# Conditioning pairs at other places, an attention step in another order, and a last step by halves

## The chip, the cores and the metric

The kernel runs on one NeuronCore of one Trainium2 chip, as one program. The metric is the time of the device in microseconds, lower is better; the kernel before took 2285.16 us, the median of three runs (2285.12 to 2285.46). Everything is float32 at the interface. A product in full precision is made as three matmuls of fp32r halves: the operand is split into a rounded part (`hi`, a cast on ACT) and the rest (`lo`, a subtraction on DVE).

## The reference

Two blocks are chained. x has 256 tokens and 1024 features.

```python
# first block
h = rms_norm(x, norm_mix)
u = h @ w_in                                   # short conv, NSA, gated delta net parts
branches = einsum('bsrc,rcd->bsrd', [y_a, y_n, y_g], w_branch)
gates    = sigmoid(h @ w_gate + b_gate)        # three branches, 1024 wide each
x = x + sum_r(gates * branches) @ w_out
x = x + hier_moe(rms_norm(x, norm_ffn), ...)   # 32 experts of 512
# second block: two layers with conditioning
mod = silu(c) @ ada_w + ada_b                  # per layer 6 x 1024: shift, scale, gate, twice
# layer 0: latent attention (MLA), 16 heads; gated FFN of 2816
# layer 1: state space (Mamba-2), 32 heads; 8 experts of 2816, 2 per token
#   x = x + gate * f(norm(x) * (1 + scale) + shift) for each of the four parts
out = rmsnorm(x, final_gain)
```

The NSA part of the first block has three attentions (compressed, selected blocks, window) over 8 heads, all with softmax over at most 256 keys.

## The kernel before

Each engine runs its own function per stage, one instruction stream each, and the streams meet only at semaphores; the order within a stream is written out by hand. Stages in order: the first block's norm, the convolution and the projections, the delta net (`gdn_*`), NSA (`nsa_*`), the merge of the branches (`merge_*`), the output projection (`proj_*`), the first mixture of experts, latent attention (`mla_*`), FFN (`ffn_*`), state space (`ssm_*`), the second mixture (`moe2`), the last norm (`last_*`).

**Weights** come through one ring of four slots (`Ring`, L103), 2 MB each. SP issues the loads in one fixed order, which is the order in which the units are written down (`columns_unit` L719, `ada_units` L724): the load of unit n waits until unit n − 4 has been emptied, and the loads behind it wait with it. A unit for a full-precision product is split into parts (`Split`, L157); `split.make_hi(a, n)` (cast, L192) and `split.make_lo(v, n)` (subtraction, L202) bring the split up to part n where they are called, and no part can be split beyond the buffers that PE has used.

**Conditioning pairs.** mod for one layer comes in 6 pairs. A pair is two ring units; `ada_pe` (L1198, its matmuls are L1209) multiplies it in 64 matmuls, `ada_act` copies the row out of PSUM (L1220), `ada_turn_pe` turns it into columns (4 small matmuls), and `ada_turn_dve` stores these into `mod_all` (L1235). There is one row buffer, so pair n + 1 is copied only when pair n is turned. In the first block's stages the pairs 3, 4 and 5 of layer 0 lie at the end of the delta net (3), after the first NSA unit (4) and ahead of the first scores (5), and pairs 1 to 5 of layer 1 in the steps 1, 3, 5, 7 and 8 of the latent attention's loop.

**Attention** (`attention_pe`, `attention_act` L1680, `attention_dve` L1703) is a loop over jobs n, shared by NSA and latent attention. ACT per step: exponentials of job n, then work put beside the loop (`beside`), then the copy of the turned probabilities of job n − 2 from PSUM (`pT`, L1700), for which PE waits before it multiplies them with the values. NSA's beside work is the merge: parts of the gates' and branches' products on PE, their hi and lo on ACT and DVE, and the gates' sigmoid (`gate_act`), which needs another activation table.

**Norms.** `norm_pe` (L922) fills PE's wait for a norm with products of constants, whose number is its last argument; `constant_products` does the same elsewhere. Their results aren't used. A norm's mean square is taken half on ACT, half on DVE; POOL makes the reciprocal root (L892, L893).

**The end.** The last down product's rows are scaled by DVE (L2448), split into hi and lo over 1024 columns, scattered to the tokens by matmuls (L252) and added to x (L2409), each an operation over the full width. Then comes the last norm, with both output tiles on DVE (L3994) and a store for each by SP.

## Time and profile before

| | us |
|---|---|
| Median of three runs | 2285.16 |
| Profiled execution, whole | 2277.89 |
| its span, first to last instruction | 2276.2 |
| PE busy in the span | 1946.6 (86%) |
| DVE busy | 1088.7 (48%) |
| ACT busy | 854.5 (38%) |
| POOL busy | 43.6 (2%) |
| Granted TensorE clock, mean | 0.955 |
| HBM read | 659.90 MB, 290 GB/s over the span |

| Stage | from | to |
|---|---|---|
| up to the projections | 0 | 112 |
| delta net | 112 | 255 |
| NSA | 255 | 423 |
| merge, output projection | 423 | 468 |
| first mixture | 470 | 952 |
| latent attention | 953 | 1117 |
| FFN | 1118 | 1319 |
| state space | 1320 | 1550 |
| second mixture | 1551 | 2267 |
| last norm | 2267 | 2276.2 |

The times of single instructions are those of the profiled execution. Idle time of an engine costs only what it delays at the next semaphore where the other engines are waiting already.

### The profile page before, as it was taken

What the parts mean: (1) busy time and instruction counts of PE and PEld (TensorE: products, weight loads), DVE (VectorE), ACT (ScalarE), POOL (GpSimd) and SP (SyncE); (2) the same over time, 40 slices, a digit from 0 to 9 for tenths busy, and PEclk for the clock granted to TensorE, in tenths of its full rate; (3) what the DMA queues carried; (4) which work ended last, traced back from release to release, by engine and by line L of the source; (5) the groups of instructions that cost most, each with busy time, mean ns of one, the idle gap of its engine ahead of it and who ended that gap; (6) DMA issues with size and microseconds to landing.
All of it is one profiled execution on the core that took longest, in us unless ns stands there. A gap on an engine that the chain in (4) does not pass through costs nothing.

```text
span 2276.2 us, 30142 instructions
## 1 busy us (share of the span) xinstructions
PE 1946.6 (86%) x12025; PEld 1394.2 (61%) x12025; DVE 1088.7 (48%) x1666; ACT 854.5 (38%) x1153; POOL 43.6 (2%) x111
## 2 busy tenths in 40 slices
PE   7989997996656666598899998998989998999997
PEld 7968776762111111266899898877665674664672
DVE  3845565432111110223555477876474573574572
ACT  4432345310000000234444357765463462463460
POOL 0010200000000000000000000000000000000000
PEclk9989998999889888899999999999999999999999
DMA  8563561579999999949555454445799999999996
GB/s 262 182 222 112 192 240 69 221 282 392 409 409 409 409 409 409 354 171 356 199 177 182 169 159 161 144 158 205 281 404 383 398 408 409 408 407 409 396 408 278
DMA packets 232012, 663.12 MB, mean 291 GB/s; under 512 B 24580, under 2 KB 33320, under 8 KB 231604
## 3 DMA queue, kind: packets, MB, share of 16 engines
q1 hardware_dynamic: 224108, 652.94, 75.4%
q10 hardware_dynamic: 7752, 8.11, 1.3%
q8 instruction: 101, 1.65, 0.3%
q14 instruction: 51, 0.42, 0.1%
HBM read 659.90 MB, written 1.10 MB: 290 GB/s over the span
## 4 chain that ended last, share of the span: by engine, by line
PE 54%; DMA 22%; DVE 13%; ACT 7%; issue 3%; POOL 0%; ACTq 0%; SPq 0%; DVEq 0%; POOLq 0%
PE psum L263 11%; PE psum L264 11%; PE psum L265 11%; PE psum L252 6%; DMA ring<-in_w_expert_down 5%; DMA ring<-in_w_expert_up 5%; DMA ring<-in_w_expert_gate 5%; PE psum L2506 4%; DMA ring<-in_moe_w_gate 3%; DVE w_lo L202 3%; PE psum L2802 3%; ACT w_hi L192 2%; PE psum L2560 2%; PE psum L1209 1%; DVE xbc L1008 1%
## 5 line engine op out<-in xcount | busy, mean ns | idle before, releaser
L202 DVE TENSOR_TENSOR w_lo<-ring,w_hi 128x1024 fp32r<-128x1024 f32 (+1 forms) x492 | 573.1, 1186 | 402.8 <-ACT w_hi L192 395.4
L192 ACT CAST w_hi<-ring 128x1024 fp32r<-128x1024 f32 (+1 forms) x492 | 497.3, 1020 | 381.2 <-PE psum L265 290.1
L2802 PE MATMUL psum<-ring,hT 128*32 128x512 f32 x960 | 147.1, 744 | 116.4 <-DMA ring<-in_w_expert_gate 63.4
L2802 PEld LDWEIGHTS psum<-ring,hT 128*32 128x32 f32 x960 | 30.3, 123 | 225.6 <-issue 88.1
L263 PE MATMUL psum<-w_hi,xg_hi 128*128 128x512 f32 (+1 forms) x384 | 147.1, 383 | 20.3 <-DVE w_lo L202 20.3
L2506 PE MATMUL psum<-ring,xg_pair 128*64 128x512 f32 (+1 forms) x768 | 155.1, 559 | 3.2 <-DMA ring<-in_moe_w_up 3.2
L2409 DVE TENSOR_TENSOR x<-x,psum 128x1024 f32<-128x1024 f32 x26 | 31.2, 1219 | 249.7 <-PE psum L252 249.7
L264 PE MATMUL psum<-w_hi,xg_lo 128*128 128x512 f32 (+1 forms) x384 | 145.1, 378 | 0.0
L265 PE MATMUL psum<-w_lo,xg_hi 128*128 128x512 f32 (+1 forms) x384 | 144.9, 377 | 0.0
L2506 PEld LDWEIGHTS psum<-ring,xg_pair 128*64 128x64 f32 x768 | 54.1, 137 | 98.9 <-issue 94.9
L2824 PE MATMUL psum<-ring,midT 128*32 128x512 f32 x480 | 69.2, 711 | 42.1 <-DMA ring<-in_w_expert_down 42.1
L263 PE MATMUL psum<-h_f_hi,w_hi 128*128 128x256 f32 x352 | 100.6, 286 | 1.8 <-DVE h_f_lo L920 1.8
L264 PE MATMUL psum<-h_f_hi,w_lo 128*128 128x256 f32 x352 | 100.4, 285 | 0.0
L265 PE MATMUL psum<-h_f_lo,w_hi 128*128 128x256 f32 x352 | 100.4, 285 | 0.0
L263 PEld LDWEIGHTS psum<-w_hi,xg_hi 128*128 128x128 f32 x384 | 73.0, 190 | 41.4 <-issue 27.7
L2560 PE MATMUL psum<-ring,midT 128*64 128x512 f32 x352 | 79.5, 596 | 7.0 <-DMA ring<-in_moe_w_down 7.0
L265 PEld LDWEIGHTS psum<-w_lo,xg_hi 128*128 128x128 f32 x384 | 72.9, 190 | 14.3
L264 PEld LDWEIGHTS psum<-w_hi,xg_lo 128*128 128x128 f32 x384 | 73.0, 190 | 13.6
L263 PE MATMUL psum<-w_hi,midT_hi 128*128 128x512 f32 x176 | 70.8, 402 | 8.6 <-DVE w_lo L202 8.6
L263 PEld LDWEIGHTS psum<-h_f_hi,w_hi 128*128 128x128 f32 x352 | 68.5, 195 | 2.2 <-DVE h_f_lo L920 2.2
L264 PE MATMUL psum<-w_hi,midT_lo 128*128 128x512 f32 x176 | 69.8, 397 | 0.0
L265 PE MATMUL psum<-w_lo,midT_hi 128*128 128x512 f32 x176 | 69.8, 396 | 0.0
(699 smaller groups left out, 3675.5 us busy)
## 6 DMA issues: line engine op xcount, KB each, us to landing
ring<-in_moe_w_down SPq DMA_DIRECT2D x176, 512.0 KB, 13.3
ring<-in_w_expert_gate SPq DMA_DIRECT2D x32, 2048.0 KB, 17.0
ring<-in_moe_w_up SPq DMA_DIRECT2D x128, 512.0 KB, 11.3
ring<-in_moe_w_gate SPq DMA_DIRECT2D x122, 512.0 KB, 12.0
ring<-in_w_expert_down SPq DMA_DIRECT2D x30, 2048.0 KB, 18.1
ring<-in_w_expert_up SPq DMA_DIRECT2D x28, 2048.0 KB, 17.6
ring<-in_ada_w SPq DMA_DIRECT2D x24, 2048.0 KB, 11.8
ring<-in_moe_w_gate SPq DMA_DIRECT2D x64, 384.0 KB, 11.3
```

Of the source, the lines that this page charges most:

```text
L192: a.copy(self.buffers(n, src.shape)[0], src).then_inc(*self.hi_made.up())
L202: v.tensor_tensor(lo, src, hi.bitcast(F32), SUB).then_inc(*self.lo_made.up())
L252: ins = p.matmul(o, l, r, start=n == 0, stop=n == len(terms) - 1)
L263: p.matmul(o, l[0], r[0], start=start, stop=False)
L264: p.matmul(o, l[1], r[0], start=False, stop=False)
L265: return p.matmul(o, l[0], r[1], start=False, stop=stop)
L1008: settle(v, v.scalar_tensor_tensor(out_, padded[:, f, j:j + T], w_cols(j), out_, MUL, ADD), st.dve, *name)
L2409: v.tensor_tensor(M.acc[:, t, :], M.acc[:, t, :], run.banks.of(st.name, "scatter", i, t), ADD).then_inc(*st.dve.up("acc", i, t))
L2506: ins = p.matmul(ps[r, cut], moe2.xg_pair[:, i - HEAVY, k0 + k, r], w[side][:, k, cut], start=k0 + k == 0, stop=k0 + k == KD - 1)
L2560: ins = p.matmul(ps[r, cut], M.midT[:, k0 + k, r], w[side][:, k, cut], start=first, stop=last)
L2802: ins = p.matmul(ps[slots_of(j), g * 512:(g + 1) * 512], M.xg[:, 2 * q + k, slots_of(j)], w[:, j, k, :], start=2 * q + k == 0, stop=2 * q ...
L2824: ins = p.matmul(ps[slots_of(j), cut], M.midT[:, q, slots_of(j)], w[:, j, cut], start=q == 0, stop=q == 3)
```

## The change

It has five parts. (1) The pairs of layer 0: pair 3 goes from the delta net's end to behind `merge_step_pe(2, 2)`, 4 from behind the first NSA unit to ahead of the first scores, 5 from there to the end of the merge; the first NSA unit is multiplied in the delta net's wait for its norm. (2) The pairs of layer 1: 1 to 3 go to steps 5, 7 and 8 of the latent attention's loop, 4 into the FFN's norm, 5 into the state-space norm; there are two row buffers instead of one; the last eighth of mod is added later, and the write and load of that layer's gate rows go into the state-space loop. The ring's order follows. (3) In NSA's loop ACT does the beside work behind the copy of the probabilities (`after=`) and not ahead of it. (4) The last down product's rows go in halves of 512 columns through scale, hi, lo, scatter and sum. (5) In the last norm, DVE multiplies the second tile by the gain while rstd is made, and ACT scales it, beside DVE's first tile.

```diff
     branch_unit(0, 1)
-    ada_units(0, 3, 4)
     columns_unit(("nsa", 0), w_in, O_Q, 512, row_parts(512))
     columns_unit(("nsa", 1), w_in, O_KV, 512, row_parts(512))
-    ada_units(0, 4, 5)
     columns_unit(("nsa", 2), w_in, O_KV + 512, 256, row_parts(256))
     gate_unit(2, 0)
     for j in range(2):
         columns_unit(("cmp", j), A["cmp_w1"][0][j], 0, 256)
+    ada_units(0, 3, 5)
     branch_unit(2, 0)
     gate_unit(2, 1)
-    ada_units(0, 5, ADA_PAIRS)
     branch_unit(2, 1)
     gate_unit(1, 0)
     gate_unit(1, 1)
     branch_unit(1, 0)
     branch_unit(1, 1)
+    ada_units(0, 5, ADA_PAIRS)
...
-        if c == 0:
-            ada_units(1, 1, 2)
-    ada_units(1, 2, ADA_PAIRS)
+    ada_units(1, 1, 4)
     for half in range(2):
         mla_out_unit(half)
+    ada_units(1, 4, 5)
...
+    ada_units(1, 5, ADA_PAIRS)
     for name, g in (("b", 0), ("c", 0), ("x", 0), ("x", 1), ("z", 0), ...
...
-        if n:
-            a.wait_ge(*st.pe.of("ada_turned", layer, n - 1))
-        a.copy(ada_row[:, 0:256], banks.of("ada", layer, n)[:, 0:256])...
+        if n >= 2:
+            a.wait_ge(*st.pe.of("ada_turned", layer, n - 2))
+        elif layer:
+            a.wait_ge(*st.pe.of("ada_turned", 0, ADA_PAIRS - 2 + n))
+        a.copy(ada_row[:, 256 * (n % 2):256 * (n % 2) + 256], banks.of("ada", layer, n)[:, 0:256])...
...
@@ gdn_pe
-        ada_pe(p, 0, 3)
+        nsa_unit_pe(p, 0)
         ps = banks.take(p, "oT")
-        constant_products(p, ps, ident, 10)
@@ gdn_act, its end
-        ada_act(a, 0, 3)
+        split.make_hi(a, split.end(unit["nsa", 0]))
@@ gdn_dve, ahead of the wait for AU
+        split.make_lo(v, split.end(unit["nsa", 0]))
@@ attention_act, behind the copy of pT
+            if after:
+                after(a, n)
@@ nsa_pe
-            if n == 0:
-                ada_turn_pe(p, 0, 3)
-                ada_pe(p, 0, 4)
...
-        ada_turn_pe(p, 0, 4)
         merge_step_pe(p, 2, 0)
...
         merge_step_pe(p, 2, 2)
+        ada_pe(p, 0, 3)
...
-        ada_pe(p, 0, 5)
+        ada_turn_pe(p, 0, 3)
+        ada_pe(p, 0, 4)
...
@@ nsa_act
-        attention_act(a, st, nsa_s, nsa_pT, nsa_mx, nsa_den, 1.0, nsa_jobs, beside=merge_beside_act)
+        attention_act(a, st, nsa_s, nsa_pT, nsa_mx, nsa_den, 1.0, nsa_jobs, after=merge_beside_act)
@@ merge_pe, its end
+        ada_pe(p, 0, 5)
@@ proj_pe
-        turned_pe(p, st, merged, KD, 13, lambda: finished(p, S["merge"]))
+        turned_pe(p, st, merged, KD, 0, lambda: finished(p, S["merge"]))
+        ada_turn_pe(p, 0, 5)
@@ mla_beside_pe
         if n == 1:
             uq_pe(p, 1)
             heads_pe(p, 1)
-            ada_pe(p, 1, 1)
...
         if n == 5:
             heads_pe(p, 3)
+            ada_pe(p, 1, 1)
+        if n == 6:
+            ada_turn_pe(p, 1, 1)
+        if n == 7:
+            ada_pe(p, 1, 2)
+        if n == 8:
+            ada_turn_pe(p, 1, 2)
             ada_pe(p, 1, 3)
+        if n == 9:
+            ada_turn_pe(p, 1, 3)
@@ ffn_pe (ssm_pe the same with pair 5, its turn behind unit b)
-        norm_pe(p, st, xn_ff, 24)
+        ada_pe(p, 1, 4)
+        norm_pe(p, st, xn_ff, 8)
...
+                if c == g == 0:
+                    ada_turn_pe(p, 1, 4)
@@ ssm_act, in the heads' loop; both are gone from before the norm's rows and behind upad b
+                if h == 9:
+                    a.wait_ge(*st.dve.of("last_gate"))
+                    gates_write_act(a, 1)
+                if h == 13:
+                    gates_load_act(a, 1)
@@ ssm_dve, ahead of the wait for daT
+        ada_turn_dve(v, 1, 5)
+        v.wait_ge(*S["ada"].dve.last())
+        v.tensor_tensor(mod[:, 40:48], mod_all[:, 88:96], colrange("ada_b_2", 88, 96), ADD)...
@@ moe2, the last down product (last_rows_act, last_scatter_pe and last_scatter_dve likewise)
+    def last_rows_dve(v):
...
+        for half in range(2):
+            cut = last_cut(half)
+            v.scalar_tensor_tensor(y_gated[:, cut], banks.of("moe2", "down", i)[:, cut], M.slot_gate[:, 0:1], gate_b[:, 1, cut],
+                                   MUL, MUL).then_inc(*st.dve.up("y_gated", i, half))
...
@@ last_dve
+        v.tensor_tensor(x[:, 1, :], x[:, 1, :], fg, MUL).then_inc(*d.up("gained"))
         v.wait_ge(*st.pool.of("rstd"))
-        for t in range(NT):
-            v.scalar_tensor_tensor(total[:, t, :], x[:, t, :], fs[:, t:t + 1], fg, MUL, MUL).then_inc(*d.up("out", t))
+        v.scalar_tensor_tensor(total[:, 0, :], x[:, 0, :], fs[:, 0:1], fg, MUL, MUL).then_inc(*d.up("out", 0))
@@ last_act
-        a.wait_ge(*S["moe2"].dve.of("acc", OUTS[-1], 0))
+        finished(a, S["moe2"])
         norm_act(a, st, total, fs)
+        a.wait_ge(*st.dve.of("gained"))
+        a.wait_ge(*st.pool.of("rstd"))
+        a.activation(total[:, 1, :], x[:, 1, :], ACT.Copy, scale=fs[:, 1:2]).then_inc(*st.act.up("out", 1))
```

## Rows read from the trace of the kernel before

**Rows 1.** Stages: length, busy PE, PEld, DVE, ACT, POOL, clock, DMA, GB/s.
```profile
255.00:423.00 168.00, 149.57 (x1024) 124.67 (x1022) 96.61 (x242) 81.92 (x171) 15.57 (x17) 0.95 0.50 173
...
953.00:1117.00 164.00, 143.63 (x1048) 108.95 (x1049) 67.02 (x148) 68.54 (x136) 2.48 (x6) 0.96 0.73 258
...
1320.00:1550.00 230.00, 213.73 (x1337) 190.84 (x1337) 174.69 (x293) 151.14 (x239) 7.43 (x10) 0.95 0.47 152
```

**Rows 2.** The page's part 4, the chain that ended last, by engine.
```profile
PE 54%; DMA 22%; DVE 13%; ACT 7%; issue 3%; POOL 0%; ACTq 0%; SPq 0%; DVEq 0%; POOLq 0%
```

**Rows 3.** All instructions of L1209, `ada_pe`; ns min/median/max.
```profile
L1209 PE MATMUL psum<-ring,cond x768: 376/379/636, 121.5 to 1077.7; 128*32 128x256 f32 x192
```

**Rows 4.** Timeline, 244 to 270: start us, us, engine, line, what.
```profile
245.38 3.66 PE L1209 MATMUL psum<-ring,cond 128*32 128x256 f32 x64
...
251.50 1.23 DVE L1625 TENSOR_TENSOR shared<-shared,os 128x1024 f32<-128x1024 f32 x1 [2.14 <-POOL os L898]
...
253.63 0.48 PE L263 MATMUL psum<-w_hi,h_mix_hi 128*128 128x512 f32 x1
...
264.71 0.50 PE L252 MATMUL psum<-ident,ada_row 128*128 128x4 f32 x4
```

**Rows 5.** Timeline of PE, 287 to 315.
```profile
293.27 3.70 PE L1798 MATMUL psum<-ring,fl 128*32 128x128 f32 x128 [0.97 <-DVE fl L1952]
...
302.48 0.33 PE L1002 MATMUL psum<-ident,nsa_s 128*128 128x128 f32 x1 [2.54 <-DVE nsa_s L1966]
...
311.04 3.66 PE L1209 MATMUL psum<-ring,cond 128*32 128x256 f32 x64
```

**Rows 6.** Timeline of SP, 287 to 330: ring loads issued.
```profile
297.03 1.36 SPq L139 DMA_DIRECT2D ring<-in_ada_w  x2
...
310.25 0.37 SPq L139 DMA_DIRECT2D ring<-in_w_branch  x1
```

**Rows 7.** DMA issues, 225 to 425: size each, median us to landing.
```profile
ring<-in_ada_w SPq DMA_DIRECT2D x4, 2048.0 KB, 10.4
```

**Rows 8.** Timeline of ACT in one attention step.
```profile
370.52 1.03 ACT L192 CAST w_hi<-ring 128x1024 fp32r<-128x1024 f32 x1
...
371.45 0.58 ACT L1700 COPY kcT<-psum 128x512 f32<-128x512 f32 x1
```

**Rows 9.** Timeline of PE in a step with a gate's sigmoid.
```profile
396.21 3.78 PE L252 MATMUL psum<-nkT,hT 128*128 128x256 f32 x8 [4.96 <-ACT dup L1700]
...
399.43 0.99 PE L263 MATMUL psum<-w_hi,h_mix_hi 128*128 128x512 f32 x1
```

**Rows 10.** Waits, 314 to 421: us in total, times, longest.
```profile
PE psum L252 <- ACT dup L1700: 9.3, 2, 5.0
```

**Rows 11.** Groups by line, 985 to 1093: busy us, mean ns, idle before.
```profile
L1209 PE MATMUL psum<-ring,cond 128*32 128x256 f32 x320 | 18.3, 380 | 2.4 <-DMA ring<-in_ada_w 2.4
```

**Rows 12.** Timeline of ACT and PE at the latent attention's end.
```profile
1079.72 3.88 ACT L192 CAST w_hi<-ring 128x1024 fp32r<-128x1024 f32 x4 [1.20 <-DMA ring<-in_mla_w_out]
...
1093.58 0.50 PE L263 MATMUL psum<-w_hi,oT_hi 128*128 128x512 f32 x1 [1.34 <-DVE oT_lo L2024]
```

**Rows 13.** Timeline of DVE and POOL in the state-space norm.
```profile
1321.81 1.22 DVE L202 TENSOR_TENSOR w_lo<-ring,w_hi 128x1024 fp32r<-128x1024 f32 x1
...
1321.86 1.74 POOL L893 TENSOR_TENSOR ss_ssm<-ss_ssm,exponent 128x2 f32<-128x2 f32 x1
```

**Rows 14.** Timeline of the end, 2260 to 2276.
```profile
2260.52 1.28 DVE L2448 SCALAR_TENSOR_TENSOR total<-psum,slot_gate,gate_b 128x1024 f32<-128x1024 f32 x1 [36.26 <-PE psum L2560]
...
2265.43 2.35 DVE L2409 TENSOR_TENSOR x<-x,psum 128x1024 f32<-128x1024 f32 x2 [1.29 <-PE psum L252]
...
2267.99 1.22 DVE L887 SCALAR_TENSOR_TENSOR total<-x 128x1024 f32<-128x1024 f32 x1 [0.21 <-DVE x L2409]
...
2269.69 0.71 POOL L893 TENSOR_TENSOR fs<-fs,exponent 128x2 f32<-128x2 f32 x1
...
2270.51 2.48 DVE L3994 SCALAR_TENSOR_TENSOR total<-x,fs,gate_b 128x1024 f32<-128x1024 f32 x2 [1.28 <-POOL fs L893]
```

More of the change, by code:

```diff
@@ L1771, in nsa_pool, with nsa_unit_pe @@
         rsqrt_pool(g, st, rc[:, :], 1.0 / 64, "rc")
+    def nsa_unit_pe(p, n):
+        u, w = unit["nsa", n], nsa_units[n][2]
+        ps = banks.take(p, "unit", u)
+        by_token_pe(p, u, h_mix, [[ps[:, t * 512:t * 512 + w] for t in range(NT)]])
     def nsa_pe(p):
@@ L1775, in nsa_pe @@
         e = st.pe
[L1776 to L1782 removed]
+        for n in (1, 2):
+            nsa_unit_pe(p, n)
         p.wait_ge(*st.dve.of("dup"))
```

113 lines of the change are left out of this document (71 added, 42 removed).

## The prediction

> **What bounds the kernel now.** I read the table of stages first, then the chain of work that ended last, then the timeline of each stage that the change touches. In [rows 1] the reader should see that no stage has one limit: TensorE is busy for 149.6 of 168 us in the sparse attention's stage, 143.6 of 164 in the latent attention's, and in the state-space stage DVE is busy for 174.7 of 230 us beside TensorE's 213.7. The chain [rows 2] is 54% TensorE, 22% DMA and 13% DVE. The DMA part is the two mixtures of experts, whose instructions the change leaves alone but for the very last step; they start earlier or later with what stands before them. So the change is worth what it is worth in five places, and I price each where it stands.
>
> **A conditioning pair.** One `ada_pe` is 64 matmuls; 768 of them make 12 pairs at a median of 379 ns each, overlapping, and one pair takes 3.66 us [rows 3, 4]. Its `ada_turn_pe` takes 0.50 us [rows 4]. It also needs two ring loads of 2 MB. No pair is removed. Only its place changes: in a wait it is free, in a stretch of continuous TensorE work it costs 4.2 us.
>
> **Place 1, from the delta net's end to the first scores.** Before, pair 3 (245.38) lies in the wait for the norm, where DVE's last product comes at 251.50 and the unit `nsa 0` begins at 253.63; the unit ends at 264.71 with a turn, and pair 4 follows (another 3.66 us) [rows 4]. After, the 11.1 us unit goes into the wait, 245.4 to 256.5, and pair 4 is gone from there. But oT, which was taken when DVE's product ended (252.7), is now taken at 256.5, and ACT's and DVE's work on it (about 3.8 us in all), and with it the next unit's split parts, come behind the unit: TensorE then sits idle for some 5.8 us, an estimate, and `nsa 1` begins near 263.2 instead of 268.7. The gain is 5.5 us there, not 11.1. Next, pair 3 goes behind `merge_step_pe(2, 2)`, in an idle time of 2.54 us [rows 5]: 1.1 us of it shows. Pair 4 replaces pair 5 ahead of the first scores (3.66 us at 311.04 [rows 5]) plus one turn, 0.5.
>
> The ring takes the gain back. Four loads of 2 MB (pairs 3 and 4) now stand ahead of `branch (2, 0)`. Before, the same kind of load was issued at 297.03, beside nothing else, and took 10.4 us at the median; the branch load was issued at 310.25 [rows 6, 7]. After, pair 4's go at the compression's end, which was 293.27 + 3.70 [rows 5] and becomes 291.5; the branch load can only go when pair 3 has emptied its slots, 2.8 us of merge products and 3.66 of pair 3 later, at about 298; it comes behind the 4 MB of pair 4 on the same queue and lands near 308, whence its first split part, which ACT makes ahead of the copies of kc, is 1 to 2.5 us later than it was. The transposes of kc, just ahead of 311.04 [rows 5], and the first scores come at about +1.5 to +3 instead of −5.5. The bounds: −5 if the load lands as fast as if alone, +4 if it waits for the last ada byte. I take +1.5, near the row of 10.4 us. (The Trainium skill, "DMA: Bandwidth & Descriptors", section "Queues, rings and completion order", has it that within one queue descriptors are consumed in ring order, which would put the branch load behind both loads of pair 4; by that alone this term would be +3.)
>
> **Place 2, the attention loop.** Per step, ACT does the exponentials, then the hi cast of a beside part (1.03 us at 370.52), then the copy of the turned probabilities (0.58 us at 371.45) [rows 8]. The cycle that sets the step is DVE's: scores, maximum, ACT's exponentials, hi, lo, finish. Putting the copy ahead of the cast delays hi, lo and the next score by 0.58 us in eight steps and, where two blocks of columns are copied, by about 1.0 in two: 8 × 0.58 + 2 × 1.0 = +6.6 if nothing is given back. Given back: in a gate's step the sigmoid and its table load stand before the copy, and TensorE waited 9.3 us in two waits for it [rows 10], 4.96 at one of them, and the full-width matmul behind it took 0.99 us against the 0.48 at a unit's usual start [rows 4, 9]. I credit 1.0 and 1.7 for these steps, since DVE's own wait is the smaller part; 1.8 at the tail, where there is no cast and the copies are early; and 1.5, an estimate, for casts that had been waiting for loads or buffers anyway (ACT is busy for only 82 of 168 us [rows 1]). Net +0.6, between −3 and +6.6. Places 1 and 2 together: +2 (−6 to +10).
>
> **Place 3, merge and projection.** Pair 5 and its turn take the place of 13 constant products and of a wait for `merged` of nearly 5 us: 3.66 us is covered by it. The output weights are asked 29 us later and land before they are wanted; the first mixture's weights are ahead by tens of us in its norm. Zero; if the cover is gone, +1.
>
> **Place 4, latent attention and the FFN.** Five pairs lie in it, 18.3 us, 2.4 of it DMA waits [rows 11]. Two of them, with their turns, stand in steps 1 to 4, where TensorE is continuous: 2 × 4.2 = 8.3 us. Three pairs stay in steps 5, 7 and 8, where pairs 3 to 5 were, so nothing is added there. Of the 8.3, about 1.5 meets waits on copies by ACT, leaving 6.8. The output weights: ACT waited 1.20 us for them at 1079.72, and the output product began at 1093.58 [rows 12]; the ring has four loads fewer before them, so they come some 6 us earlier too, against a wait of about 1 us for the pair in step 8 in place of one of the same size. −6.8, between −2 (loads late) and −9. Pair 4 goes ahead of the FFN's norm in place of constants, hidden in 7 us; its turn behind the first unit is not: +0.5. ACT's copy of it waits behind the norm and delays nobody.
>
> **Place 5, state space.** Pair 5 is hidden in its norm as above. Its turn costs TensorE 0.5 us, and DVE's copy and addition some 0.4 on a chain that DVE sets there; the two writes of gate rows and the load (1 MB) move from the norm, where they hid, into head steps 9 and 13 on ACT, which is shorter than DVE but not by much. +0.7, between 0 and +2.
>
> **Place 6, the end.** Before: gated rows 2260.52 (1.28), hi, lo, scatter, accumulate 2265.43 to 2267.78, mean 2267.99 (1.22), two POOL operations, outputs 2270.51 (2.48) [rows 14]. By halves, the chain of full-width operations becomes half of the first, then half steps: the last accumulate ends near 2265.9 (−1.8), both means near 2267.3. Both outputs side by side save 1.24; the second store is issued next to the first, +0.4 and some contention. But DVE's `x1 *= fg` reads two SBUF operands while POOL makes rstd. In the state-space norm POOL's second operation, started beside a lo subtraction of DVE (1321.81 to 1323.03), took 1.74 us and ended 0.57 after it [rows 13]; the same operation at the end, alone, took 0.71 [rows 14]. So rstd is 0.8 to 1.0 later. Sum: −1.9 − 1.2 + 0.95 + 0.65 = −1.5, between −2.5 and 0. (The Trainium skill, "SBUF — State Buffer", on the shared port pair: a DVE operation with two SBUF inputs and a GpSimd operation exclude each other for a whole instruction. By it this edit pays up to a whole 1.22 us; the row agrees with it.)
>
> **Sum.** +2 + 0 − 6.8 + 0.5 + 0.7 − 1.5 = −5.1. The profiled execution of 2277.89 us (span 2276.2) would become 2272.8; it stands 7.3 us under the median of 2285.16, and I carry the difference over: 2285.16 − 5.1 = **2280.1 us**. About 0.2% (4.6 us) is what a measurement of this kernel can tell from no change, so the forecast lies at that edge.
>
> **The rivals.**
> - *Attention keeps its early start* (0.22): the branch load lands in time and the copies fill waits of ACT. For it: DVE and ACT are both idle for over half of the stage. Against it: the queue. Places 1 and 2 give −4.5 in place of +2: 2273.6.
> - *Attention pays in full* (0.12): the copies' 6.6, less 0.7 for the shorter tail, and +2 from the branch: +7.9 in place of +2, 2286. For it: DVE's cycle has ACT in series.
> - *Slower, by the clock* (0.14): one mechanism. New idle times of TensorE (5.8 us near 257, 5 to 7 near 305) drop the granted clock to its lower level, 1.2 GHz, for what follows, as after the 4.96 us wait [rows 9]; it decides if the work behind the new idle times runs as the row behind the 4.96 us one. Some 5 us of matmuls at half speed after each: +2.5 twice, on top of the copies in full (6.6 less 0.7) and a branch wait of 3.6: +14.5 in place of +2, 2292.6.
> - *The latent attention gives nothing back* (0.10): the pairs' loads, issued only as ring slots empty, arrive late at steps 7 and 8, or another wait ends these steps. −2 in place of −6.8: 2284.9.
> - The forecast, 0.42, with its own range 2276 to 2284 from the bounds of single places; a little over 0.6 of it lies below 2280.6.
>
> **How the numbers follow.** Faster by over 0.2%: 0.22 + 0.42 × 0.63 = 0.48. Within: 0.12 + 0.10 + the rest of the forecast's, 0.16 = 0.38; slower 0.14. The range leaves out half of the clock's case and the better end of the first rival: 2272.5 to 2288.5.
>
> **What would show it.** Unit `nsa 1` about 5.5 us earlier, after an idle time of 5 to 6 us; the ada loads of pair 4 issued near 291 and the branch load near 298; the first scores at 314.6 + 1 to 3. In the loop, the hi cast behind the copy, and TensorE's waits for the copy at gates shorter. The output product of latent attention 6 to 7 us earlier against its stage's start. At the end, a POOL operation of over 1 us beside the product with fg. The prediction is wrong if the first scores come 4 us early, if the loop is over 4 us longer or shorter, or if the latent stage gives under 4 us.

## The result, and the profile after

The changed kernel takes **2290.25 us** (median of 10 runs, 2286.03 to 2294.21), the kernel before 2285.21 in the same rounds: a ratio of 1.0026 with a 95% interval of 1.0016 to 1.0036. (Three executions of two versions below fell in a slow state, with 2575 to 6424 us, and the medians leave them out.) The changed kernel is slower by about 5 us where 5 us of gain were forecast, and lies above the stated range. The profiled execution took 2289.63 us with a span of 2287.8.

The profiled execution of the kernel before stands 7.3 us under its median, that of the changed kernel 0.6 under its own. So both kernels were profiled a second time (2288.42 us and a span of 2286.7 for before; a span of 2286.3 for the changed one). The marks between the stages are POOL's first operations on the norms' sums. Timeline of POOL in the changed kernel (start us, us, engine, line, what):

```profile
250.52 0.21 POOL L895 TENSOR_SCALAR os<-os 128x8 f32<-128x8 f32 x1 [125.92 <-DVE os L1624]
...
478.84 0.22 POOL L891 TENSOR_SCALAR ss_ffn<-ss_ffn 128x2 f32<-128x2 f32 x1 [164.56 <-DVE xn_ffn L886]
...
964.99 0.24 POOL L891 TENSOR_SCALAR ss_mla<-ss_mla 128x2 f32<-128x2 f32 x1 [0.99 <-DVE mod L3088]
...
1123.06 1.05 POOL L891 TENSOR_SCALAR ss_ff<-ss_ff 128x2 f32<-128x2 f32 x1 [130.32 <-DVE silf L886]
...
1325.15 0.24 POOL L891 TENSOR_SCALAR ss_ssm<-ss_ssm 128x2 f32<-128x2 f32 x1 [200.24 <-DVE mod L3088]
...
1561.15 0.22 POOL L891 TENSOR_SCALAR ss_moe<-ss_moe 128x2 f32<-128x2 f32 x1 [0.81 <-ACT xn_moe L873]
...
2280.05 1.24 POOL L891 TENSOR_SCALAR fs<-fs 128x2 f32<-128x2 f32 x1 [717.88 <-DVE total L886]
```

With the same marks in all four profiles, and the starts of the first scores and the end of the last down product on PE:

| stretch, us | before, twice | changed, twice | difference of the means | predicted |
|---|---|---|---|---|
| delta net's root to first scores | 65.1, 66.4 | 72.6, 73.7 | +7.4 | +1.5 |
| first scores to the first mixture's root (loop, merge, projection) | 156.6, 154.8 | 155.7, 155.7 | 0.0 | +0.6 |
| first mixture | 483.7, 486.1 | 486.2, 486.5 | +1.4 | 0 |
| latent attention | 164.8, 166.9 | 158.1, 158.3 | −7.6 | −6.8 |
| FFN | 201.8, 200.8 | 202.1, 202.1 | +0.8 | +0.5 |
| state space | 231.4, 235.4 | 236.0, 237.6 | +3.4 | +0.7 |
| second mixture | 707.6, 710.2 | 711.1, 708.3 | +0.8 | 0 |
| last down product to the end | 15.7, 15.7 | 15.6, 15.5 | −0.1 | −1.5 |

What is missing up to the spans' difference of 5.6 us (−0.4) lies ahead of the delta net's root. The two profiles of before differ by 10.5 us in span: 5.0 of it lies in the two mixtures, 4.0 in the state space and 2.0 in the latent attention. The first alone would have shown a loss of 11.6 us, twice the 5.6 of the means. A difference of under 2 us in one stage of single profiles, or of 4 in the state space, is therefore no finding by itself.

The first loss is ahead of the attention. Timeline of the changed kernel, PE, SP and ACT, 263 to 324, with the idle time before an instruction and its releaser in brackets:

```profile
263.98 0.77 PE L263 MATMUL psum<-w_hi,h_mix_hi 128*128 128x512 f32 x1 [5.58 <-DVE w_lo L202]
...
265.39 0.63 PE L263 MATMUL psum<-w_hi,h_mix_hi 128*128 128x512 f32 x1
...
293.85 0.99 SPq L139 DMA_DIRECT2D ring<-in_ada_w  x2
...
300.42 0.37 SPq L139 DMA_DIRECT2D ring<-in_w_branch  x1
...
311.31 1.04 ACT L192 CAST w_hi<-ring 128x1024 fp32r<-128x1024 f32 x1 [6.96 <-DMA ring<-in_w_branch]
...
315.56 0.26 PE L1823 MATMUL psum<-ident,kc 30*64 30x30 f32 x1 [8.18 <-DVE kc L1972]
...
316.06 1.01 PE L252 MATMUL psum<-ident,ada_row 128*128 128x4 f32 x4
...
317.01 6.17 PE L1208 MATMUL psum<-ring,cond 128*32 128x256 f32 x64
...
323.11 1.06 PE L252 MATMUL psum<-kcT,hT 128*128 128x15 f32 x8
```

`nsa 1` begins 13.5 us behind the root (250.52) instead of 19.2 (249.52 to 268.74 in the kernel before), as forecast. But its first products run at half the clock. From 263.98 to 267.52 there are 8 of them, one every 0.44 us, where the later ones follow each other every 0.23: 1.7 us of the start are lost again, and everything behind them, the ring's loads included, is that much later. Windows there (length, busy PE, PEld, DVE, ACT, POOL, granted clock, DMA share, GB/s):

```profile
264.00:268.00 4.00, 4.00 (x11) 3.15 (x12) 3.24 (x3) 1.74 (x2) 2.80 (x3) 0.56 0.00 0
268.00:272.00 4.00, 4.00 (x19) 3.30 (x18) 2.22 (x2) 1.65 (x2) 0.00 (x0) 1.00 0.85 288
```

Then the branch's load, issued at 300.42 behind pair 4's two, is what ACT's cast waits for, 6.96 us; the copies of kc stand behind that cast, and PE idles for 8.18 us until 315.56. In the kernel before it stood idle for 1.12 us there:

```profile
310.68 0.21 PE L1820 MATMUL psum<-ident,kc 30*64 30x30 f32 x1 [1.12 <-DVE kc L1971]
```

Counted from the root, these transposes come 3.9 us later than before (65.0 against 61.2). And pair 4, which takes 3.66 us elsewhere [rows 4, 5], takes 6.17. The landing times (DMA issues of 292 to 304, median us to landing) and the windows of the same stretch:

```profile
ring<-in_ada_w SPq DMA_DIRECT2D x2, 2048.0 KB, 11.8
...
ring<-in_w_branch SPq DMA_DIRECT2D x1, 1024.0 KB, 10.9
```
```profile
300.00:310.00 10.00, 7.38 (x55) 5.78 (x47) 0.00 (x0) 3.37 (x5) 0.00 (x0) 1.00 1.05 388
310.00:315.00 5.00, 0.00 (x0) 0.00 (x0) 2.35 (x2) 2.50 (x6) 1.20 (x2) 0.69 0.94 345
315.00:320.00 5.00, 4.44 (x36) 2.56 (x39) 1.77 (x5) 1.43 (x4) 0.00 (x0) 0.50 0.03 11
320.00:325.00 5.00, 5.00 (x52) 3.11 (x45) 0.64 (x6) 1.66 (x2) 0.00 (x0) 0.79 0.14 10
```

From 300 to 315 the DMA engines are full (345 to 388 GB/s): from 293.85 on the queue has 7 MB to bring (pair 4, the branch's and the gate's weights), and no load is slow by itself. Pair 4's two loads, issued at 293.85 and 294.26, land 9.3 and 14.3 us later, at 303.1 and 308.5; the branch's lands at 311.3, behind both. And behind the idle time the granted clock is 0.50, the lower of the two levels.

The second loss is in the state space. Timeline of PE, and windows at the same place:

```profile
1392.49 0.80 PE L263 MATMUL psum<-w_hi,h_ssm_hi 128*128 128x512 f32 x1 [5.69 <-ACT upad L3667]
```
```profile
1384.00:1389.00 5.00, 2.80 (x24) 2.59 (x22) 4.86 (x14) 3.15 (x6) 0.00 (x0) 1.00 0.45 167
1389.00:1394.00 5.00, 1.51 (x4) 1.23 (x5) 3.74 (x7) 4.32 (x6) 0.00 (x0) 0.65 0.16 52
1394.00:1399.00 5.00, 5.00 (x17) 3.94 (x16) 4.43 (x10) 1.71 (x4) 0.00 (x0) 0.67 0.46 138
```

PE waits 5.69 us for ACT's copy `upad`. Before, this wait doesn't exist. The code says why: PE's results go to four pairs of PSUM banks in rotation, but in the state-space stage a table, written by hand, fixes the pairs from unit z 0 on (`("z", 0): 1`). The pair that a use ahead of that takes depends on how many uses came before it and on those that were held. Followed through both kernels, in order of the takes: before, pair 1 was last used by unit x 0 when z 0 takes it; in the changed kernel it was last used by x 1, the unit just multiplied, whose copy is the one waited for.

The end, timeline of DVE, POOL, ACT and SP:

```profile
2273.72 1.35 DVE L2480 TENSOR_TENSOR ysb_lo<-total,ysb_hi 128x512 fp32r<-128x512 f32 x2
...
2274.88 0.48 PE L252 MATMUL psum<-ysb_hi,selgT 128*128 128x512 f32 x1
...
2276.09 2.35 DVE L2505 TENSOR_TENSOR x<-x,psum 128x1024 f32<-128x1024 f32 x2 [1.02 <-PE psum L252]
...
2279.99 1.23 DVE L4058 TENSOR_TENSOR x<-x,gate_b 128x1024 f32<-128x1024 f32 x1
2280.05 1.24 POOL L891 TENSOR_SCALAR fs<-fs 128x2 f32<-128x2 f32 x1 [717.88 <-DVE total L886]
...
2281.37 0.71 POOL L892 TENSOR_TENSOR fs<-fs,exponent 128x2 f32<-128x2 f32 x1
2282.12 1.29 DVE L4060 SCALAR_TENSOR_TENSOR total<-x,fs,gate_b 128x1024 f32<-128x1024 f32 x1 [0.91 <-POOL fs L892]
2282.18 1.15 ACT L4068 ACTIVATE total<-x,fs 128x1024 f32<-128x1024 f32 x1 [2.42 <-POOL fs L892]
2283.44 0.84 SPq L4109 DMA_DIRECT2D out<-total  x2
```

### The profile page after: what moved, and what is told of

It is laid out like the page before. It is cut to its first block, busy times and chain, and to the rows that moved or that the text cites. A ratio compares the mean times of both kernels' runs of the same rounds, so it can differ in the third digit from the quotient of the medians.

```text
span 2287.8 us, 29926 instructions
## 1 busy us (share of the span) xinstructions
PE 1943.8 (85%) x11913; PEld 1384.7 (61%) x11913; DVE 1089.2 (48%) x1669; ACT 855.5 (37%) x1155; POOL 45.0 (2%) x111
## 4 chain that ended last, share of the span: by engine, by line
PE 55%; DMA 22%; DVE 11%; ACT 7%; issue 3%; SPq 1%; POOL 0%; ACTq 0%; POOLq 0%; DVEq 0%
PE psum L263 12%; PE psum L264 11%; PE psum L265 11%; PE psum L252 7%; DMA ring<-in_w_expert_up 6%; DMA ring<-in_w_expert_down 5%; DMA ring<-in_w_expert_gate 5%; PE psum L2557 4%; DMA ring<-in_moe_w_gate 3%; PE psum L2859 2%; DVE w_lo L202 2%; ACT w_hi L192 2%; PE psum L2611 2%; PE psum L1208 1%; PE psum L2881 1%
## 5 line engine op out<-in xcount | busy, mean ns | idle before, releaser
L2557 PE MATMUL psum<-ring,xg_pair 128*64 128x512 f32 (+1 forms) x768 | 155.3, 559 | 3.2 <-DMA ring<-in_moe_w_up 3.2
L263 PEld LDWEIGHTS psum<-w_hi,xg_hi 128*128 128x128 f32 x384 | 73.9, 192 | 42.0 <-issue 28.0
L265 PEld LDWEIGHTS psum<-w_lo,xg_hi 128*128 128x128 f32 x384 | 73.9, 192 | 14.5
L264 PEld LDWEIGHTS psum<-w_hi,xg_lo 128*128 128x128 f32 x384 | 73.9, 192 | 13.9
L263 PE MATMUL psum<-h_mix_hi,w_hi 128*128 128x256 f32 x224 | 64.0, 286 | 7.0 <-DVE w_lo L202 7.0
```

The costliest lines, as they stand in the source:

```text
L263: p.matmul(o, l[0], r[0], start=start, stop=False)
L264: p.matmul(o, l[1], r[0], start=False, stop=False)
L265: return p.matmul(o, l[0], r[1], start=False, stop=stop)
L2557: ins = p.matmul(ps[r, cut], moe2.xg_pair[:, i - HEAVY, k0 + k, r], w[side][:, k, cut], start=k0 + k == 0, stop=k0 + k == KD - 1)
```

## The experiments

All ran beside the kernel before, whose own median moved from set to set of runs (2283.05 to 2285.98 us), so versions of different sets are compared by their difference to it, in the third column, or by the ratio. "Root" is the mark at the delta net's norm. Theory: the loss is (a) the queue ahead of the attention, (b) the clock behind the wait it makes, (c) the PSUM pair of z 0. Rivals: the attention's new order, the moves of layer 1, and chance of the execution. All single stages below are of one profile each.

| version | median us | minus before, same runs | ratio to before, 95% | root to scores | scores to first mixture | latent | state space | down to end |
|---|---|---|---|---|---|---|---|---|
| changed | 2290.25 | +5.0 | 1.0026 [1.0016, 1.0036] | 72.6 | 155.7 | 158.1 | 236.0 | 15.6 |
| changed, second set of runs | 2291.82 | +6.9 | 1.0026 [1.0015, 1.0037] | 73.7 | 155.7 | 158.3 | 237.6 | 15.5 |
| dt takes pair 3 | 2295.78 | +9.8 | 1.0037 [1.0023, 1.0050] | 73.7 | 155.8 | 158.0 | 244.5 | 15.6 |
| branch load first | 2287.16 | +1.2 | 1.0009 [1.0000, 1.0018] | 67.0 | 158.9 | 158.3 | 236.3 | 15.6 |
| cast first, as before | 2289.90 | +3.9 | 1.0018 [1.0007, 1.0029] | 73.6 | 155.3 | 158.2 | 239.0 | 15.5 |
| layer 1's moves alone | 2280.39 | −5.3 | 0.9974 [0.9963, 0.9985] | 66.5 | 156.0 | 162.8 | 232.4 | 15.7 |
| and pair 5 in the merge | 2277.01 | −8.7 | 0.9962 [0.9949, 0.9976] | 63.4 | 155.7 | 158.2 | 234.1 | 15.7 |
| pair 3 behind oT | 2273.44 | −12.2 | 0.9944 [0.9930, 0.9958] | 61.2 | 157.5 | 158.0 | 232.9 | 15.7 |
| x 0 takes pair 1, last norm as before | 2283.64 | −2.0 | 0.9989 [0.9980, 0.9999] | 73.9 | 155.7 | 158.2 | 235.8 | 14.6 |
| x 0 takes pair 1 | 2285.74 | +2.7 | 1.0013 [1.0003, 1.0022] | 72.7 | 158.0 | 158.7 | 234.9 | 15.6 |
| 60 constant products in the wait | 2291.50 | +8.5 | 1.0037 [1.0024, 1.0049] | 74.7 | 156.8 | 158.3 | 236.0 | 15.6 |
| 34 constant products in the wait | 2284.40 | −0.5 | 0.9994 [0.9985, 1.0002] | 70.4 | 155.7 | 158.5 | 238.0 | 15.6 |
| pair 3 behind oT, halves | 2273.27 | −9.8 | 0.9955 [0.9941, 0.9969] | 62.2 | 155.5 | 158.1 | 232.8 | 14.6 |
| the same, copy first | 2275.14 | −7.9 | 0.9964 [0.9953, 0.9976] | 61.1 | 158.4 | 158.1 | 231.7 | 14.6 |

**The PSUM pair, first try.** Edit on the changed kernel:

```diff
-        ps = banks.take(p, "dt")
+        ps = banks.take(p, "dt", pair=3)
```

> The changed kernel with one edit: the state-space stage's dt product takes PSUM pair 3, so that unit z 0, whose pair 1 is fixed by a table, again follows unit x 0 and not x 1 on that pair. Theory (the change has shifted the rotation of the four PSUM pairs, and TensorE waits 5.7 us for ACT's copy of x 1 out of the pair that z 0 needs): that wait at 1392 goes, the state-space stage is 3.5 to 4.5 us shorter than in the changed kernel (236.0 us from one norm's root to the next), and the median is 3 to 4.5 us lower. Rival (the stage is longer because of the turn, DVE's addition and the moved gate rows): the stage stays within 1 us of 236.

The wait of z 0 went, and the stage grew to 244.5 us. PE's waits, 1330 to 1570 (us in total, times, longest), and the windows behind:

```profile
PE psum L1001 <- ACT xbc L3698: 3.8, 1, 3.8
PE psum L259 <- ACT ada_row L1221: 3.2, 1, 3.2
```
```profile
1330.00:1340.00 10.00, 6.77 (x35) 6.40 (x35) 5.12 (x9) 5.87 (x10) 0.00 (x0) 0.69 1.05 392
1340.00:1350.00 10.00, 10.00 (x48) 10.00 (x48) 0.84 (x4) 0.26 (x1) 0.00 (x0) 0.50 0.44 160
```

Pair 3 had been pair 5's (conditioning) bank, emptied late by ACT: a new wait of 3.2 us, and then 10 us and more at the lower clock level (0.50), in which PE was busy without a gap. The expectation (3.5 to 4.5 us shorter) failed because the edit moved the wait instead of removing it; it shows what a wait of 3 us can cost.

**The queue.** Edit on the changed kernel:

```diff
-    ada_units(0, 3, 5)
+    ada_units(0, 3, 4)
     branch_unit(2, 0)
+    ada_units(0, 4, 5)
```

> The changed kernel with one edit in the ring's order: the load of branch (2, 0) stands ahead of pair 4's two loads and behind pair 3's. Theory (this 1 MB load, third in the queue behind 4 MB, lands 10.9 us after its issue, ACT stands 7 us at its cast ahead of the copies of kc, TensorE idles for 8.2 us and then runs at half clock): the cast runs before 303, the transposes of kc come near 307 instead of 315.6, the first scores at 314 to 316 instead of 323.1, and 6 to 9 us of the median go. Rival (pair 4's loads, now issued behind it, come as late and TensorE waits in pair 4 instead): first scores at 320 or later and under 3 us gained.

The cast no longer waits and the transposes of kc come at 307.14, as expected. The scores come 5.6 us earlier against the root, at 315.3. Part of the rival happened too: pair 4 now waits for its own weights and is slow behind that wait. PE's row, and the waits of 310 to 434:

```profile
310.03 5.35 PE L1209 MATMUL psum<-ring,cond 128*32 128x256 f32 x64 [1.93 <-DMA ring<-in_ada_w]
...
ACT w_hi L192 <- DMA ring<-in_w_gate: 7.3, 1, 7.3
PE psum L252 <- ACT dup L1702: 3.9, 2, 2.0
```

Now the gate's load stands behind pair 4's, and ACT waits 7.3 us for it; the stretch of loop, merge and projection is 3.2 us longer (158.9 against 155.7). Some of that may be chance: a version below whose code is the changed kernel's in this stretch has 158.0 in its one profile. Against the kernel before, the time went from +5.0 to +1.2, so about 4 us were gained where 6 to 9 were expected. So the order is one part of it; the other is that pairs 3 and 4 bring 8 MB into a stretch that had 4 MB of pair 5 in it, with the queue full from 300 to 315.

**The order in the loop.** Edit on the changed kernel:

```diff
-        attention_act(a, st, nsa_s, nsa_pT, nsa_mx, nsa_den, 1.0, nsa_jobs, after=merge_beside_act)
+        attention_act(a, st, nsa_s, nsa_pT, nsa_mx, nsa_den, 1.0, nsa_jobs, beside=merge_beside_act)
```

> The changed kernel with ACT's order in the NSA loop as before: the beside work ahead of the copy of the turned probabilities. By the prediction's step (net cost of the new order +0.6 us) it is within 1 us of the changed kernel. Rival A (each step's cast is later by the copy, with little given back): 4 to 6 us faster. Rival B (the copy ahead of the sigmoid gives back more than it costs): 2 us or more slower, with TensorE's two waits of some 5 us for the copy back at the gates.

The kernel before is exceeded by 3.9 us instead of 5.0, with intervals of the ratio that overlap, and the profile has 155.3 against 155.7. The prediction's net of +0.6 is within this; it is smaller than these runs can tell from nothing, but the 4 to 6 us of rival A appear in neither measure. Inside, the loop is 2.0 us shorter with the cast first (107.9 against 109.9) and the merge 1.6 longer. PE's waits for the copy, of this version and of the changed kernel, show that the copy first does what it is meant for:

```profile
PE psum L252 <- ACT dup L1701: 8.6, 2, 5.0
```
```profile
PE psum L252 <- ACT dup L1701: 2.9, 2, 1.9
```

**The kernel before, again.**

> The kernel before, unchanged, for a second profile. The profiled execution shown of it took 2277.89 us, 7.3 under its median, while that of the changed kernel took 2289.6, 0.6 under its own. If the difference of the two mixtures of experts between the two profiles (+2.4 and about +3.5 us) is a matter of the execution and not of the change, this profile has the mixtures near the longer times (486 and 711 us) and a span nearer 2283; if it belongs to the change, they are again near 483.4 and 707.5.

The mixtures took 486.1 and 710.2 us: execution, not change. The span was 2286.7.

**Layer 1 alone.** The kernel before with the moves of layer 1's pairs; all else as before.

```diff
     for c in range(2):
         columns_unit(("uq", c), A["mla_w_uq_2"][0], 768 * c, 768)
         columns_unit(("ukv", c), A["mla_w_ukv_2"][0], 1024 * c, 1024)
-        if c == 0:
-            ada_units(1, 1, 2)
-    ada_units(1, 2, ADA_PAIRS)
+    ada_units(1, 1, 4)
...
```

> The kernel before with the moves of layer 1's pairs alone (latent attention, FFN and state-space norms, two row buffers, gate rows in the heads' loop); layer 0, the attention's order and the end are those of before. Theory (these moves give what was predicted and the loss lies in layer 0): the latent attention's stage, from root to root of the norms, is 157 to 159 us against 164.8 and 166.9 in the two profiles of before, the state-space stage within 1 us of 235.4, and the median 5 to 8 us under the kernel before. Rival (the state-space stage pays for the moves): over 238 us there, and under 4 us gained.

2280.39 us, −5.3: at the lower end of the 5 to 8 expected. In its profile the latent stage was 162.8 and not under 159: set beside the next version, which shares this code, PE keeps step up to 1080 and then falls back by 5 us behind a wait of 2.8 us for the probabilities, with a granted clock of 0.59 in the window of 1077.7 to 1087.7. The thirteen other profiles with this code have 158.0 to 158.7. The state space did not pay (232.4).

**And pair 5 in the merge.** On that, as in the changed kernel, the loads of pair 5 going behind the merge's in the ring. One more edit came with it, `banks.turn = 1` ahead of unit x 0 of the state space, which is shown further down:

```diff
-        ada_pe(p, 0, 5)
         p.wait_ge(*st.act.of("vc"))
...
             banks.let_go("unit", unit["branch", 1, half])
+        ada_pe(p, 0, 5)
```

> The same, and pair 5 of layer 0 at the end of the merge as in the changed kernel, with pairs 3 and 4 where they were before. Theory: the first scores come 3 to 4.5 us earlier against the delta net's root (62.5 us instead of 66.4), because a pair leaves the path and 4 MB leave the queue ahead of the attention; the merge's stage is no longer; the median is 8 to 12 us under the kernel before. Rival (the gates' products, no longer delayed by the pair, wait for other weights, or the merge pays): under 2 us more than the moves of layer 1 alone. PSUM pair of x 0 set so that z 0 follows x 0, as before.

The scores came 3.1 us earlier (63.4 against 66.5), the merge took the pair at no cost, the median fell by another 3.4. 8 to 12 us under the kernel before were expected and 8.7 measured. The other edit doesn't show as a gain (state space 234.1 against 232.4: without it, this code has no wait for `upad` either).

**Pair 3 behind oT.** On the changed kernel, with the order of the loop and the end as before, and again with `banks.turn = 1`:

```diff
     columns_unit(("nsa", 0), w_in, O_Q, 512, row_parts(512))
+    ada_units(0, 3, 4)
     columns_unit(("nsa", 1), w_in, O_KV, 512, row_parts(512))
...
-    ada_units(0, 3, 5)
+    ada_units(0, 4, 5)
     branch_unit(2, 0)
...
+        ada_pe(p, 0, 3)
         for n in (1, 2):
             nsa_unit_pe(p, n)
...
         merge_step_pe(p, 2, 2)
-        ada_pe(p, 0, 3)
+        ada_pe(p, 0, 4)
```

> The changed kernel's delta net end (first NSA unit in the norm's wait), but pair 3 directly behind oT, where the changed kernel's TensorE was idle for 5.6 us, pair 4 behind merge step (2, 2), pair 5 in the merge; ACT's order in the loop and the end as before; PSUM pair of x 0 set. Theory (a pair in each real wait, at most two loads of a pair ahead of the branch's): nsa 1 starts within 1.5 us of the changed kernel's 13.5 us after the root, the first scores 57 to 60 us after it against 66.4 before and 72.6 changed, the median 12 to 17 us under the kernel before. Rival (DMA: the loads up to the first gate are the limit of this stretch, whatever the order): first scores later than 62 us after the root.

2273.44 us, 12 under the kernel before. The rows of PE at the delta net's end and of SP:

```profile
257.93 3.66 PE L1209 MATMUL psum<-ring,cond 128*32 128x256 f32 x64
...
265.39 0.79 PE L263 MATMUL psum<-w_hi,h_mix_hi 128*128 128x512 f32 x1 [3.80 <-ACT q L1849]
```
```profile
276.16 10.83 SPq L139 DMA_DIRECT2D ring<-in_ada_w  x2
295.80 0.37 SPq L139 DMA_DIRECT2D ring<-in_w_branch  x1
```

Pair 3 fits into the idle time the changed kernel had (5.58 us ahead of 263.98), and `nsa 1` begins 15.3 us behind the root against 13.5. At 265.39, behind 3.80 us of idle time, a product takes 0.79 us again. The scores come at 61.2, 1.2 us later than the upper end expected. The rival (the loads are the limit, whatever the order: over 62) isn't excluded, as the two versions below that share this stretch have 62.2 and 61.1. What is shown is the gain: 65.1 and 66.4 in the kernel before.

**The PSUM pair again, and the last norm.** Two edits in different stages of the changed kernel:

```diff
+        banks.turn = 1
         by_feature_pe(p, unit["ssm", "x", 0], h_ssm)
...
-        v.wait_ge(*d.of("mean"))
-        v.tensor_tensor(x[:, 1, :], x[:, 1, :], fg, MUL).then_inc(*d.up("gained"))
         v.wait_ge(*st.pool.of("rstd"))
-        v.scalar_tensor_tensor(total[:, 0, :], x[:, 0, :], fs[:, 0:1], fg, MUL, MUL).then_inc(*d.up("out", 0))
+        for t in range(NT):
+            v.scalar_tensor_tensor(total[:, t, :], x[:, t, :], fs[:, t:t + 1], fg, MUL, MUL).then_inc(*d.up("out", t))
```

> The changed kernel with two edits in different stages. First, x 0 takes PSUM pair 1 (and x 1 pair 2), so that z 0 waits for the copy of x 0, long done, and no operation ahead of it gets a new wait: theory, TensorE's 5.7 us wait goes, and the stage is 1 to 4 us shorter than 236.0; rival (another wait ends the stretch, as DVE's chain sets it): within 0.7 us of 236.0. Second, the last norm as before (both output tiles on DVE, no product beside POOL), the last step still by halves: theory (the lock of POOL costs what the two tiles side by side bring), POOL's first operation takes 0.22 us again instead of 1.24, and from it to the end it is 6.8 us instead of 7.75, so the end is 0.9 to 1.1 us earlier; rival (the second tile on DVE costs as much): within 0.2 us of 7.75.

The end, POOL's timeline:

```profile
2278.81 0.22 POOL L891 TENSOR_SCALAR fs<-fs 128x2 f32<-128x2 f32 x1 [716.96 <-DVE total L886]
2279.11 0.71 POOL L892 TENSOR_TENSOR fs<-fs,exponent 128x2 f32<-128x2 f32 x1
```

0.22 us instead of 1.24, and from there to the end 6.8 us instead of 7.75: DVE's product beside POOL, with the two tiles side by side, costs 1 us more than it brings. The state space was 235.8 in this profile, with a wait for the convolution in the place of the 5.7 us:

```profile
PE psum L1001 <- ACT xbc L3699: 4.2, 1, 4.2
```

Against the kernel before, both edits together went from +5.0 to −2.0, 7 us and more than the 1.0 of the end. So the first edit was tried alone:

```diff
+        banks.turn = 1
         by_feature_pe(p, unit["ssm", "x", 0], h_ssm)
```

> The changed kernel with one edit: x 0 of the state-space stage takes PSUM pair 1, so that z 0 does not wait for ACT's copy of x 1. Theory (this wait, and the half clock behind it, cost the state-space stage 2 to 4 us, though the profile with two edits did not show it): median 2 to 5 us under the changed kernel's 2290.25, near 2286. Rival (the wait only changes its name, 4.2 us for the convolution instead): within 1 us of 2290.25 in the median.

2285.74 us. That is 2.7 us above the kernel before of the same runs, where the changed kernel is 5.0 and 6.9 above its own: 2.3 to 4.2 us less, as expected, though the intervals of the ratios overlap (1.0003 to 1.0022, and 1.0016 to 1.0036). The profile has 234.9. The six profiles with z 0's wait have 236.0, 237.6, 236.3, 239.0, 236.0 and 238.0 (mean 237.1); the seven without it and with the moves, leaving out the version whose dt waits, have 232.4, 234.1, 232.9, 235.8, 234.9, 232.8 and 231.7 (mean 233.5), and the two of before 231.4 and 235.4 (mean 233.4). No value of the second kind reaches one of the first, the nearest by 0.2. The 3.6 us between the means are not all the wait's, however. The two versions that differ from the changed kernel ahead of and in this stage by the one edit are the 235.8 and the 234.9, 1.8 us under the six. The five others, with a mean of 232.8, also differ in layer 0, and why they are shorter still is not shown.

**The wait filled.** Edit on the changed kernel, first with 60 and then with 34 products:

```diff
-        p.wait_ge(*st.dve.of("kc"))
         ps = banks.take(p, "kcT2")
+        constant_products(p, ps, ident, 60)
+        p.wait_ge(*st.dve.of("kc"))
```

> The changed kernel with 60 constant products (some 7 us) ahead of TensorE's wait for kc, in the 8.2 us in which it stood idle at 307. Nothing is moved, and nothing waits for them. Theory (the granted clock falls in that idle time, and pair 4 behind it takes 6.17 us instead of 3.66): pair 4 takes 3.7 to 4.2 us, its turn 0.5, the first scores come 2.5 to 3.5 us earlier against the root (69 to 70 instead of 72.6), median 2 to 3 us lower. Rival (pair 4 is slow for another reason, its weights still landing): 6 us as before, no gain.

The 60 took 13.56 us and reached past the wait, so the scores were 1 to 2 us later and not 2.5 to 3.5 earlier, and the time rose to 8.5 us above the kernel before. But pair 4 behind them took 3.66 us. It also began 4.6 us later against the root than in the changed kernel, so this run alone doesn't exclude the rival of late weights.

> The same with 34 constant products. The run with 60 showed that a product's group takes 0.226 us (13.56 us for 60), twice what was reckoned, so they reached 5 us past the wait; pair 4 behind them took 3.66 us at full clock. 34 of them are 7.7 us, inside the 8.2. Theory (the granted clock, and nothing else, made pair 4 and its turn slow): transposes of kc at 315.0 to 315.8 as in the changed kernel, pair 4 in 3.7 us, first scores near 320 instead of 323.1, and the median 2 to 4 us lower. Rival (time won there is lost in the loop, where the gate's weights are the limit): first scores earlier, but the merge begins as late as in the changed kernel.

Timeline of PE:

```profile
306.99 7.75 PE L259 MATMUL psum<-ident 128*128 128x128 f32 x68
...
315.52 0.21 PE L1824 MATMUL psum<-ident,kc 30*64 30x30 f32 x1 [0.78 <-DVE kc L1973]
...
316.41 3.66 PE L1208 MATMUL psum<-ring,cond 128*32 128x256 f32 x64
...
320.00 1.06 PE L252 MATMUL psum<-kcT,hT 128*128 128x15 f32 x8
```

The transposes of kc come as late as in the changed kernel. Pair 4 starts no later than there (19.9 us behind pair 3's start, against 20.3) and takes 3.66 us, so its weights were not what made it slow, and the stretch from kc to the scores is 4.5 us instead of 7.6: the clock behind this idle time was 3.1 us of the loss. Nothing of it was given back in the loop and merge (155.7 both). The median is 7.4 us under the changed kernel of the same rounds, more than the profile's 3.1 accounts for; where the other 4 lie, no profile of these runs shows.

**The changed kernel, again.**

> The changed kernel, unchanged: a second profile, and its time in the same rounds. Theory (the 236.0 us of the state-space stage belong to the wait for x 1's copy and the clock behind it, as in the other kernels with this code: 236.3, 239.0, 236.0, against 235.8, 234.9, 232.4, 234.1, 232.9, 232.8 and 231.7 without that wait): 236 us or more again. Rival (chance of the execution): under 235. The stretch from the delta net's root to the first scores is again 72.6 within 1 us in every case, as in the kernels that share it (72.7 and 73.6).

237.6 us in the state space, 73.7 from root to scores: as the theory had it.

**Put together.** The version with pair 3 behind oT, with the last step by halves kept, and the last norm as before. Against the version without the halves:

```diff
-        scatter_pe(p, run2, OUTS[-1])
+        last_scatter_pe(p)
...
+        if i == OUTS[-1]:
+            last_rows_dve(v)
+            return
...
-        scatter_dve(v, run2, OUTS[-1])
+        last_scatter_dve(v)
```

> The version with pair 3 directly behind oT and the last norm as before, and with it the last step by halves. Theory: the halves alone bring the 1.1 us seen between the last down product and the root (7.8 us instead of 8.9) and nothing is given back, since no product stands beside POOL: median 1 us (0 to 2) under the version without them, about 2272.4; 12 to 15 us under the kernel before. Rival: the halves are lost in the last norm's wait, no difference.

2273.27 us, ratio 0.9955 (0.9941 to 0.9969). The profile has the halves' 1.1 us (7.8 us from the last down product to POOL's root instead of 8.9); the median doesn't show them. It was expected 1 us under the version without halves; against the kernel before it gains 9.8 us where that one gained 12.2, with intervals that overlap. The same with the copy first in the loop (`after=` for `beside=` in the call of `attention_act`):

> The version with pair 3 behind oT and the halves, with the changed kernel's order in the NSA loop (the copy of the probabilities ahead of the beside work). By the comparison in the changed kernel (loop +2.0 us, merge -1.6): within 1 us of the version without it. Rival: it shows its worth only where the weights of the gates are there in time: 2 us or more faster.

2275.14 us, no difference that these runs can tell (loop, merge and projection 158.4 against 155.5 in single profiles; the version without halves, with the same loop as the 155.5, has 157.5).

## Why the prediction was wrong

**What held.** The latent attention (−6.8 predicted, −7.6 measured, and −5.3 in the median with layer 1's moves alone), the loop and merge with the new order (+0.6, measured 0.0; the edit alone 0.4 in the profile), pair 5 hidden in the merge, the FFN (+0.5, +0.8), the idle time ahead of `nsa 1` (5.8, 5.58), POOL beside DVE's product (0.95, 1.02).

**Place 1, the largest error (+1.5 predicted, +7.4 measured).** The mechanism was named: the ring takes the gain back, ACT's cast stands ahead of the copies of kc. The step that failed is the clock, which the forecast's own terms put at nothing. It put full-clock time behind two idle times of PE that I had myself worked out, 5.8 us ahead of `nsa 1` and 5 to 7 us ahead of kc. In the first pair of profiles the error is 6.0 us, and by the rows it comes apart like this. Behind the first idle time the unit loses 1.7 us; by that, pair 4's loads are issued 43.3 us behind the root instead of the 42.0 that 291.5 means, so 1.4 us late. Behind the second the clock takes 3.1 us, which the run with 34 products shows. The remaining terms are small: 0.9 for the landing of the branch's load, and 0.5 for the turn, which the prediction names but +1.5 doesn't hold. That the first 1.4 us reach the scores is read from rows; no run tests it.

On the landing: I took 10 us from the issue at 298 to 308, by the 10.4 us of an ada load that had the queue to itself. It took 10.9 with the DMA engines full. The load did wait for the last byte of pair 4 (308.5, and 311.3 for the branch's), which I had called a bound, as the Trainium skill's rule on descriptors consumed in ring order ("DMA: Bandwidth & Descriptors", "Queues, rings and completion order") would have had it. What made the transposes of kc 3.7 us later than before, in the mean of two profiles each, and not 1.5, was for the larger part that all of this began late.

I kept the clock for a rival of 0.14, with 2.5 us for each such place; the runs show 1.7 and 3.1. The rival was the right mechanism at nearly the right price, and the prediction names nothing that speaks against it. The row on which it rested, 0.99 us for a matmul behind a 4.96 us wait [rows 9], should have gone into the forecast's own terms. That the rival's 2292.6 lies near the measured time is luck all the same: it charges 5.9 us for the copies, which cost nothing measurable, and has nothing for the losses of places 5 and 6.

**Place 5 (+0.7, +3.4).** The step that failed is a term put at nothing without a reason: that moving a conditioning pair changes which PSUM pair every later product takes. I priced each moved instruction, its load and its queue, and not the rotation, although the table that fixes the pairs from z 0 on was in the code. In its place stands a wait of 3.7 to 6.2 us for `upad`, in all six profiles with it. Taking it out is worth 1.8 us in the profiles and 2.3 to 4.2 in the medians; the rest of the +3.4 stays open, since the two profiles of before stand 4.0 us apart. The moved pairs' own cost is about nothing as far as the means tell (233.5 without the wait, 233.4 before).

**Place 6 (−1.5, −0.1).** The halves gave 1.1 and not 1.9: the scatter of the first half starts at 2274.88, half a us behind its lo part (2273.72 + 0.67), with the constant products put there for the full-width step still running; and ACT's and DVE's squares both now wait for the last sum. The lock was right. The outputs side by side gave nothing: the first store is issued 0.14 us earlier against the last product than before, and it is 4.36 us from there to the end where it was 4.38. The second store is issued 0.9 us earlier against the last product than before, but beside the first it lands 3.5 us after its issue instead of 2.7. Taking the last norm back is worth 1.0 us.

**The sum.** Errors of 5.9, 2.7 and 1.4 us in the three places make 10.0 of the 10.1 us between −5.1 and +5.0; the rest (latent attention, loop, FFN, the start and the scatter of the mixtures) comes to +0.7 in the profiles. The range was too narrow at its upper end, 2288.5, because it left out half of the clock's case, which had 0.14. The bounds of places 1 (+4) and 5 (+2) hold no clock either, and 7.4 and 3.4 were measured: at the first, part of the loss is what the clock takes behind a wait of PE. One sum was also wrong: the bounds of places 1 and 2 together are −8 to +10.6, not −6 to +10.

## What to carry to other kernels

Work moved into a wait of the tensor engine brings its loads along: count the megabytes that stand in the queue ahead of the next weights that are needed, and put the move where the wait is and the queue is empty, not only where the wait is. A wait of the tensor engine can cost more than its length (here 3.1 us on top of 8.2, and 1.7 on top of 5.6), because what runs behind it may run at half clock; fill what can't be removed, with work sized so that it ends inside. When anything is added to or taken from a rotation of buffers, follow the rotation to every place that pins a buffer by hand.

## What the runs showed of the hardware

The clock can stay at its lower level for long behind a short wait: in the version whose dt waited, behind waits of 1.9 and 3.2 us in the norm, ten us of PE work without a gap (1340 to 1350) ran at a clock of 0.50. At a granted clock of 1.00 a constant product of 128 columns takes 0.226 us and shows as two records (13.56 us and 120 records for 60). A POOL operation of 2 columns beside a DVE product with two SBUF operands took 1.24 us instead of 0.22, ending 0.07 us after the product (2279.99 + 1.23), which agrees with the Trainium skill's account of a lock on a shared port pair ("SBUF — State Buffer", "Who interferes with whom"). Two stores of 512 KB issued 0.4 us apart landed 2.7 and 3.5 us after their issue, and 2.7 both when they were issued 1.2 us apart.
